# Low parts of the side weights made by ScalarE and an adding DMA from GpSimd, in place of a VectorE subtraction

## Time and profile before

| | before |
|---|---|
| median of 3 runs | 2506.87 us (2506.82 to 2506.97) |
| span of the profiled execution | 2505.1 us |
| TensorE busy | 2490.8 us, 99% |
| TensorE weight loads | 2204.3 us, 88% |
| VectorE busy | 1961.7 us, 78% |
| ScalarE busy | 1232.5 us, 49% |
| GpSimd busy | 305.3 us, 12% |
| granted TensorE clock | 1.00 |
| DMA | 246.87 MB, 33.9% of 16 engines on SP's queue |

### The profile page before, as it was taken

The page is one execution under the profiler, slowest core; times in us unless marked ns, Lnnn a source line. Parts: engine busy times, 40 slices in busy tenths (PEclk is TensorE's granted clock), DMA queues, the critical chain, the costliest instruction groups (busy, mean ns, idle before and its releaser), DMA issues.

```text
span 2505.1 us, 37038 instructions
## 1 busy us (share of the span) xinstructions
PE 2490.8 (99%) x14548; PEld 2204.3 (88%) x14548; DVE 1961.7 (78%) x2794; ACT 1232.5 (49%) x1963; POOL 305.3 (12%) x250
## 2 busy tenths in 40 slices
PE   9999999999999999999999999999999999999998
PEld 7999988889999889999888899998888888899997
DVE  7878867778888688887777888876899786877663
ACT  6444445444444454444553544445577535644442
POOL 4000001320000000000023100000187221200002
PEclk9999999999999999999999999999999999999999
DMA  5333332223333423333323233334333333233331
GB/s 157 98 96 100 100 105 84 82 85 102 96 108 102 118 79 104 96 106 114 102 64 95 74 103 105 104 104 135 91 72 82 126 92 111 83 108 99 99 100 59
DMA packets 487299, 246.87 MB, mean 99 GB/s; under 512 B 42321, under 2 KB 483926, under 8 KB 486870
## 3 DMA queue, kind: packets, MB, share of 16 engines
q1 hardware_dynamic: 486674, 244.19, 33.9%
q10 hardware_dynamic: 452, 0.32, 0.1%
HBM read 240.27 MB, written 4.19 MB: 98 GB/s over the span
## 4 chain that ended last, share of the span: by engine, by line
PE 96%; DVE 2%; ACT 1%; DMA 0%; issue 0%; POOL 0%; DVEq 0%; ACTq 0%
PE bank L886 8%; PE bank L885 8%; PE bank L884 8%; PE bank L767 6%; PE bank L768 6%; PE bank L769 6%; PE psS L906 4%; PE psS L907 4%; PE psS L908 4%; PE psT L950 2%; PE psT L952 2%; PE psT L951 2%; PE psT L767 2%; PE psT L769 2%; PE psT L768 2%; PE bank L1449 1%
## 5 line engine op out<-in xcount | busy, mean ns | idle before, releaser
L2254 DVE TENSOR_TENSOR wlo<-raw,whi 128x1024 fp32r<-128x1024 f32 (+2 forms) x212 | 288.7, 1364 | 49.9 <-ACT whi L1575 46.7
L767 PE MATMUL bank<-xhi,whi 128*128 128x512 f32 x672 | 264.5, 394 | 0.0
L768 PE MATMUL bank<-xlo,whi 128*128 128x512 f32 x672 | 261.9, 390 | 0.0
L769 PE MATMUL bank<-xhi,wlo 128*128 128x512 f32 x672 | 261.8, 390 | 0.0
L884 PE MATMUL bank<-xsh,whi 128*128 128x256 f32 x840 | 237.8, 283 | 0.0
L885 PE MATMUL bank<-xsl,whi 128*128 128x256 f32 x840 | 237.7, 283 | 0.0
L886 PE MATMUL bank<-xsh,wlo 128*128 128x256 f32 x840 | 237.7, 283 | 0.0
L1575 ACT ACTIVATE whi<-raw 128x1024 fp32r<-128x1024 f32 (+2 forms) x209 | 214.5, 1030 | 39.1 <-PE bank L769 22.1
L2317 DVE TENSOR_TENSOR wlo<-tw,whi 128x1024 fp32r<-128x1024 f32 x140 | 171.6, 1226 | 63.4 <-ACT whi L1615 63.3
L906 PE MATMUL psS<-hhi,whi 128*128 128x512 f32 x488 | 191.7, 393 | 0.0
L907 PE MATMUL psS<-hlo,whi 128*128 128x512 f32 x488 | 191.6, 393 | 0.0
(11 more groups left out here) (709 smaller groups left out, 7280.5 us busy)
## 6 DMA issues: line engine op xcount, KB each, us to landing
raw<-in_ffn_wg SPq DMA_DIRECT2D x88, 512.0 KB
raw<-in_ffn_wu SPq DMA_DIRECT2D x88, 512.0 KB
raw<-in_w_in SPq DMA_DIRECT2D x53, 512.0 KB
raw<-in_w_mlp SPq DMA_DIRECT2D x40, 512.0 KB
raw<-in_ffn_wd SPq DMA_DIRECT2D x48, 256.0 KB
raw<-in_ffn_wd SPq DMA_DIRECT2D x24, 448.0 KB
raw<-in_ffn_wd SPq DMA_DIRECT2D x48, 192.0 KB
raw<-in_ffn_wd SPq DMA_DIRECT2D x48, 128.0 KB
```

Of the source, the lines that this page charges most:

```text
L767: pe.matmul(dest, a, rhs_hi(k), start=start and k == 0, stop=False)
L768: pe.matmul(dest, a, rhs_lo(k), start=False, stop=False)
L769: mm = pe.matmul(dest, b_, rhs_hi(k), start=False, stop=stop and k == tiles - 1)
L2254: dve.tensor_tensor(wlo[:, a:a + n], raw[:, a:a + n], whi[:, a:a + n].bitcast(F32), ALU.subtract).then_inc(s_split, 1)
```

## The change

VectorE's `whole_lo` goes, in the networks and the MLP. Right behind `whole_hi`, ScalarE writes a second pass over the same raw columns, scaled by -1, into `wlo`: the negated high part. GpSimd then issues a DMA that adds the raw columns to it in place, from SBUF to SBUF, so that `wlo` holds raw minus high. There is one such DMA for each side, 164 in all; it waits for the pass by `k_nh`, and its landing raises `k_sl[0]` or `k_sl[1]` by 16. TensorE waits for that before a side; SP waits for it before it loads the next rows into the slot, since the DMA reads `raw` till then. VectorE's other increments of `s_split` are raised so that the count of four per window stays (`weight_sums` adds 2 from the second window on, the first split after the windows adds 2); `k_lo` counts three per window. GpSimd's DMA loop stands before the mixing stage of each layer, after its sums of squares, and before the last norm's sums for the MLP.

To have semaphores for this, four of the memory's norm are merged with four of the attention's v path, with offsets in their waits; that moves no instruction.

```
 def side_rows(w, i):                          # SP
     slot_free(c, q0)
+    if w:
+        sp.wait_ge(k_sl[i], 16 * (net.first_g + w))
...
 for m in range(KC):
+    if m in (2, 3):
+        sp.wait_ge(k_sl[m - 2], 16 * (net.first_g + FAST))
     down_rows(LAST_AT + m, -1, m)
...
 def fast_window(w):                           # TensorE
-    pe.wait_ge(k_lo, 4 * g + 1)
+    pe.wait_ge(k_lo, 3 * g + 1)
...
-    pe.wait_ge(k_lo, 4 * g + 3)
+    pe.wait_ge(k_sl[0], 16 * (g + 1))
     side(w, 0).then_inc(s_used, 1)
...
-    pe.wait_ge(s_split, q + c + 4 + RING)
+    pe.wait_ge(k_sl[1], 16 * (g + 1))
     side(w, 1).then_inc(s_used, 1)
...
 def whole_hi(j, i):                           # ScalarE
     act.activation(whi[:, a:a + n], raw[:, b_:b_ + n], ACT.Copy).then_inc(s_hi, 1)
+    act.activation(wlo[:, a:a + n], raw[:, b_:b_ + n], ACT.Copy, scale=-1.0).then_inc(k_nh, 1)
...
 def weight_sums(j):                           # VectorE
-    dve.tensor_tensor(tw[:, 3 * S:4 * S], raw[:, S:UNIT], tw[:, 0:S], ALU.subtract).then_inc(s_split, 1)
+    dve.tensor_tensor(tw[:, 3 * S:4 * S], raw[:, S:UNIT], tw[:, 0:S], ALU.subtract
+                      ).then_inc(s_split, 2 if j else 1)
...
-def whole_lo(j, i):
-    dve.wait_ge(s_hi, q0 + c0 + 4 * (PLAIN + j) + 2 + 2 * i)
-    a, b_, n = (2 * i + 1) * UNIT, (2 + i) * UNIT, side_cols(j, i)
-    dve.tensor_tensor(wlo[:, a:a + n], raw[:, b_:b_ + n], whi[:, a:a + n].bitcast(F32),
-                      ALU.subtract).then_inc(s_split if i else k_lo, 1)
...
+def sides_lo(first, cols):                    # GpSimd
+    for w in range(len(cols)):
+        for i in range(2):
+            a, b_, n = (2 * i + 1) * UNIT, (2 + i) * UNIT, cols[w][i]
+            pool.wait_ge(k_nh, 2 * (first + w) + i + 1)
+            pool.dma_start(wlo[:, a:a + n], raw[:, b_:b_ + n], accum_op=ALU.add).then_inc(k_sl[i], 16)
...
 for l in range(0, L):
+    net_sides_lo(2 * l)
     mix(l)
     squares(l * 3 + 2)
+    net_sides_lo(2 * l + 1)
...
+sides_lo(FIRST_G, [[len(MSIDES[w, i]) * P for i in range(2)] for w in range(MFAST)])
 squares(FINAL1 + 3, FINAL1 + 3, KC - 1, more=1)
```

More of the change, by code:

```diff
@@ L332, in build @@
         a_os = sem("attn_out_low_rest")
[L333 to L336, removed]
+        s_vs = sem("v_scaled_or_mem_normed")
+        s_vt = sem("v_or_mem_transposed")
+        s_vh = sem("vhi_ready_or_mem_squared_or_root")
+        s_vl = sem("vlo_ready_or_mem_newton_step")
         s_qs = sem("qk_scaled")
@@ L450, in build @@
         k_lo = sem("fast_weights_lo_ready")
+        k_nh = sem("side_weights_hi_negated")
+        k_sl = [sem(f"side_weights_lo_landed{i}") for i in range(2)]
         k_pe = sem("fast_product_done")
@@ L480, in build @@
         assert (C_MLP + WINDOWS_AT) % RING == 0
+        SIDE_SLOTS = (2, 3)
         FIRST_G, FIRST_ADD = sum(net.fast for net in NETS), 2 * L * ADDS
@@ L727, in mlp_side_rows @@
                 slot_free(c, 0)
+                if w > 0:
+                    sp.wait_ge(k_sl[i], 16 * (FIRST_G + w))
                 chunks = sorted({(grp, m) for grp, m, k in MSIDES[w, i]})
@@ L746, in _ @@
             for m in range(KC):
-                load(C_MLP + MLAST_AT + m, 0, c2(t["w_mlp2_2"], *MGROUPS[-1], m * P))
+                c = C_MLP + MLAST_AT + m
+                slot_free(c, 0)
+                if slot(c) in SIDE_SLOTS and m < RING:
+                    sp.wait_ge(k_sl[SIDE_SLOTS.index(slot(c))], 16 * (FIRST_G + MFAST))
+                sp.dma_start(dst(c, 0, mlp_tiles(-1)), c2(t["w_mlp2_2"], *MGROUPS[-1], m * P)
+                             ).then_inc(landed[slot(c)], LANDED)
             ov = out.rearrange("o (i p) d -> p (o i) d", p=P)
@@ L1303, in _ @@
                     r = m // 5
-                    pe.wait_ge(s_mn, MB)
+                    pe.wait_ge(s_vs, L + MB)
                     if r:
@@ L1312, in _ @@
                                               memr[:, j * D + cc * P:j * D + (cc + 1) * P], ident[:, :])
-                    mm.then_inc(s_mt, 1)
+                    mm.then_inc(s_vt, 1)
             def cross_q(h, ready=None):
@@ L1485, in mlp_window @@
                 mlp_terms(bank_d, cwh, cwl, S, mlp_corner(4, 0), True, True).then_inc(k_pe, 1)
-                pe.wait_ge(k_lo, 4 * g + 2)
+                pe.wait_ge(k_lo, 3 * g + 2)
                 pe.wait_ge(k_sn, 3 * g + 1)
@@ L1495, in mlp_window @@
                 mlp_terms(bank_c, whi, wlo, S, mlp_summed(0), True, True).then_inc(s_used, 1)
-                pe.wait_ge(k_lo, 4 * g + 4)
+                pe.wait_ge(k_lo, 3 * g + 3)
                 pe.wait_ge(k_sn, 3 * g + 2)
                 mlp_terms(bank_a, whi, wlo, 2 * UNIT, mlp_summed(2), False, True, True).then_inc(k_pe, 1)
-                pe.wait_ge(k_lo, 4 * g + 3)
+                pe.wait_ge(k_sl[0], 16 * (g + 1))
                 mlp_side(w, 0).then_inc(s_used, 1)
@@ L2035, in _ @@
                                            accum_out=st2[:, 16 + i:17 + i])
-                    e.then_inc(s_mr, 1)
-                    act.wait_ge(s_mst, 1)
-                    act.activation(st2[:, 20:22], st2[:, 18:20], ACT.Sqrt).then_inc(s_mr, 1)
+                    e.then_inc(s_vh, 1)
+                    act.wait_ge(s_vl, L + 1)
+                    act.activation(st2[:, 20:22], st2[:, 18:20], ACT.Sqrt).then_inc(s_vh, 1)
                 if m in (3, 6):
                     r = m // 6
-                    act.wait_ge(s_mt, r + 1)
+                    act.wait_ge(s_vt, L + r + 1)
                     for i in range(4):
@@ L2249, in _, with split @@
         def _(dve):
-            def split(c, q, tiles=8):
+            def split(c, q, tiles=8, units=1):
                 dve.wait_ge(s_hi, q + c + 1)
@@ L2333, in ahead @@
                     elif u == 4 * PLAIN + 1:
-                        whole_lo(0, 0)
+                        pass
                     elif u == 4 * PLAIN + 2:
@@ L2338, in ahead @@
                     else:
-                        split(c0 + u, q0, UNIT_TILES.get(u, 8))
+                        split(c0 + u, q0, UNIT_TILES.get(u, 8), 2 if u == LAST_AT else 1)
                 def quarter_sums(i):
@@ L2424, in fast_window @@
                     side_adds(w, 0)
-                    if on:
-                        whole_lo(w + 1, 0)
-                    else:
+                    if not on:
                         ahead(u + 5)
@@ L2906, in _ @@
                     v, y = st2[:, 18:20], st2[:, 20:22]
[L2907 to L2910, removed]
+                    dve.wait_ge(s_vh, L + 1)
+                    dve.tensor_scalar(v, st2[:, 16:18], 1.0 / D, EPS, ALU.mult, ALU.add).then_inc(s_vl, 1)
+                    dve.wait_ge(s_vh, L + 2)
+                    dve.reciprocal(y, y).then_inc(s_vl, 1)
                     for j in range(2):
[L2912 to L2918, removed]
+                        dve.wait_ge(s_vl, L + j + 2)
+                        dve.tensor_tensor(v, v, y, ALU.mult).then_inc(s_vl, 1)
+                    dve.wait_ge(s_vl, L + 4)
+                    dve.tensor_scalar(v, v, -0.5, 1.5, ALU.mult, ALU.add).then_inc(s_vl, 1)
+                    dve.wait_ge(s_vl, L + 5)
+                    dve.tensor_tensor(y, v, y, ALU.mult).then_inc(s_vl, 1)
+                    dve.wait_ge(s_vl, L + 6)
                     for i in range(MB):
                         mr = memr[:, i * D:(i + 1) * D]
-                        dve.tensor_scalar(mr, mr, st2[:, 20 + i:21 + i], None, ALU.mult).then_inc(s_mn, 1)
+                        dve.tensor_scalar(mr, mr, st2[:, 20 + i:21 + i], None, ALU.mult).then_inc(s_vs, 1)
                 if m in (3, 6):
@@ L3071, in mlp_sums_lo @@
                                   ALU.subtract).then_inc(k_lo, 1)
[L3073 to L3077, removed]
             def mlp_last_lo(j):
@@ L3086, in mlp_ahead @@
                 elif u < MLAST_AT + KC:
-                    split(C_MLP + u, 0)
+                    split(C_MLP + u, 0, 8, 2 if u == MLAST_AT else 1)
             def mlp_quarter_sums(i):
@@ L3138, in mlp_window @@
                 mlp_side_adds(w, 0)
-                if on:
-                    mlp_whole_lo(w + 1, 0)
-                else:
+                if not on:
                     mlp_ahead(MLAST_AT + 1)
@@ L3179, in _ @@
             mlp_hidden_lo(MPLAIN - 2, tmp[2])
-            mlp_whole_lo(0, 0)
             mlp_sums_lo(0, 1)
@@ L3313, in _, with net_sides_lo @@
             pool.wait_ge(s_ro, 13)
+            def sides_lo(first, cols):
[4 more added lines that the diff above has]
+                        pool.dma_start(wlo[:, a:a + n], raw[:, b_:b_ + n], accum_op=ALU.add).then_inc(k_sl[i], 16)
+            def net_sides_lo(nf):
+                net = NETS[nf]
+                sides_lo(net.first_g, [[net.side_cols(w, i) for i in range(2)] for w in range(net.fast)])
             for l in range(0, L):
+                net_sides_lo(2 * l)
                 mix(l)
                 squares(l * 3 + 2)
+                net_sides_lo(2 * l + 1)
             pool.wait_ge(s_x, (FINAL1 + 1) * KC)
```

14 lines of the change are left out of this document (4 added, 10 removed).

## The result

The changed kernel takes 2510.78 us (median of 20 runs, 2510.58 to 2511.05) against 2506.89 us before (20 runs, 2506.70 to 2507.15): +3.9 us, a ratio of 1.0016 with a 95% interval of 1.0009 to 1.0022. That is inside the 0.2% that the prediction counts as no change, but on the slower side, 3.8 us above the forecast of 2507.0, and its interval leaves out a ratio of 1. The span went from 2505.1 to 2509.0 us.

A forecast was written before the change was run, and what follows sets the result against it. TensorE, busy 2490.8 of 2505.1 us, was taken as the bound. Sum: 2505.1 + 0 (VectorE) + 0.1 (ScalarE in the MLP) + 0 (transfers) + 1.8 outside the span = 2507.0 us, no change; range 2505.3 to 2512.9 us.

The forecast's parts named there:

- VectorE: Side subtractions removed, 114.4 us of VectorE time beside a TensorE that never waits for it: gain 0, at best 1.6 us.
- The rival in which it reaches the end: VectorE's relief closes more than its own four waits: 2505.3 us by those waits; chance of over 0.2% faster 0.03.
- ScalarE in the networks: Second pass for side 1 delays the copy of TensorE's first block to 211.68, wanted at 212.18: hidden by 0.5 us, cost 0.
- ScalarE in the MLP: Copy behind the second pass ends 0.11 us before the third block; bounds 0 and 1.1 us over 11 windows, 0.1 taken.
- Transfers: 164 adding DMAs from GpSimd land before TensorE wants the low part: cost 0, at the upper bound about 6.0 us.
- L: Time from the end of ScalarE's second pass to the transfer's landing: 5.5 us, between 2.5 and 9.4.
- GpSimd's own share: GpSimd's part of the time from second pass to landing: 1.4 us, between nothing and 2.8 us.
- Loads: SP's queue waits for landings and transfers slow weight loads by at most 1.8 us; VectorE's weight sums covered by 6.6: cost 0.
- The late landing: Rival: landing exceeds what TensorE leaves; nothing to 7.8 us, every window pays beyond 10.8, 2663 us at 12; chance 0.06.
- hold GpSimd up: Rival: GpSimd writes descriptors only while VectorE idles, delaying side 0's transfer start by 5.7 us: 2520 us, chance 0.03.
- The first DMA: Rival: GpSimd's queue setup lengthens TensorE's first wait and moves everything one for one: 2512 us, chance 0.02.
- Windows still without a wait of TensorE: Sign that the prediction is right: in the windows, TensorE still shows no waits after the change.

The follow-up runs named there:

- late_all: Changed kernel with ScalarE's second pass for side 1 moved behind the copies TensorE waits for, in all windows including the first ones: 2506.43 us, ratio 0.9998 to before.
- late_first: Changed kernel with ScalarE's second pass for side 1 moved behind the next corner's pass and third block's copy in the four first windows alone: 2508.86 us, ratio 1.0008.
- double_dma: Changed kernel with each of the 164 adding transfers issued twice, the second after the first landed, TensorE and SP waiting for the second: 2523.18 us, ratio 1.0075.
- dma_alone: Changed kernel with its transfers but without ScalarE's second pass; VectorE writes the negated high part instead: 2506.43 us, ratio 0.9998 to before.
- double_other: Against double_dma, the second transfer adds the high part instead of the raw weights, and SP waits only for the first landing: 2560.77 us, ratio 1.0212.

## Why the prediction was right or wrong

**VectorE: right.** Its relief gave nothing: late_all has it, and its time can't be told from that of the kernel before. The rival in which it reaches the end did not happen.

**ScalarE in the networks: the term that failed.** The prediction gave 0, "hidden by 0.5 us", from one window, and that window follows one with four tiles in side 1. The same working on the window at 674, 674.76 + 2 x 0.61 + 0.37 = 676.35, ends 0.15 us past the third block's start at 676.20: 2.1 us in 14 windows. Measured, 2.4. That the two are so close is in part luck: the passes overlap, so the copy ends some 0.2 us earlier than this sum has it, and TensorE starts 0.15 us after the copy's end, not at it. The mechanism, the copy behind the pass, was named; what failed was to let one window stand for 66, in which the copy of the changed kernel ends between 0.14 and 0.86 us ahead of the third block. For the first windows the prediction worked out the transfer alone and left out what stands behind the pass on ScalarE there: 2.15 us by the starts, 1.9 us by late_first.

**The range: held by luck.** The measured time lies inside it, but its high end stands on late landings in the first windows (6.0 us), which did not happen. What filled 3.8 us of it is ScalarE in the networks, to which the sum gave 0 without bounds.

**ScalarE in the MLP: right, at the better bound.** 0.1 taken, 0 measured. The pass began 0.09 us before the one ahead of it had ended, as the prediction took into account when it chose, and the copy 0.10 us before the pass had; so the copy ends 0.35 us ahead of the third block, where the sum without overlap had it 0.11.

**Transfers: right, and near in size.** L, from the end of the pass to the landing, was 5.5 us with bounds of 2.5 and 9.4; it measures 3.2 to 6.4 us, in the middle 3.8 (side 0) and 4.7 (side 1). GpSimd's own share was the mis-sized half, 1.4 us taken; issue begins 0.29 us after the pass, and what follows takes 4.2 (4.1 taken). TensorE's first use of a side comes at least 4.3 us after the landing. The estimate of 2.6 us by the Trainium skill's page "DMA: Bandwidth & Descriptors" (section "Anatomy of one DMA — SWDGE (gpsimd) path") is too low for an adding transfer within SBUF: 4.1 us for 256 KB in the trace, and the measurement decides.

**Loads: right that they cost nothing, wrong about the cover.** SP waited for landings 67 times in the networks, and TensorE not once for what followed. But one more transfer, some 4 us, already cost 12.4 us, through the very chain for which the prediction gave 6.6 us of cover.

**The rivals.** The late landing did not happen; its price curve, nothing until 7.8 us, is too kind, since the loads give way before TensorE meets the landing (double_dma). VectorE did not hold GpSimd up: the issue follows the pass by 0.29 to 0.62 us, while VectorE is as busy as before but for the subtractions it no longer makes. That two-tensor operations leave GpSimd free to write descriptors is what the Trainium skill's page "SBUF — State Buffer" (section "Who interferes with whom") says, with its reason marked as inferred; the 0.29 us, and 0.85 to 1.06 us for every DMA instruction, agree. The first DMA cost no start: TensorE's first wait is 3.8 us as before.

**The signs to look for.** "Windows still without a wait of TensorE" was too coarse a test: the 14 stalls appear in no view of waits. VectorE 114 us lighter and ScalarE 104 us heavier took sums of groups for busy time; measured, 96.4 and 78.3.

## What to carry to other kernels

Work added to an engine with room is hidden only where nothing queued behind it is due: take the cover from the window that has the least of it, not from one that is at hand, and look for it where two lengths that vary (here a short side, then a long one) meet. The remedy is then order, not less work: the pass, moved behind the copies that TensorE waits for, cost nothing any more (late_all). And a loss near nothing can mark a cover that has just run out; doubling the suspect (3.9 us, then 46 us) shows it.

## What the runs showed of the hardware

An adding transfer from SBUF to SBUF, issued by GpSimd, keeps it 0.86 us and lands 2.9 to 6.1 us later, in the middle 4.1 us for 192 KB and 4.4 us for 512 KB: over this range the size hardly shows. The DMA engines' mean share over the windows of the first network goes up from 0.35 to 0.53 by these transfers (dma_alone), and that kernel lost no time that can be measured.

TensorE's granted clock fell after a wait. In double_other TensorE waited 2.25 us for a landing, until 262.50. Busy time of the engines in the stretches before, during and after (the columns as in the earlier trace rows):

```profile
256.00:259.90 3.90, 3.90 (x30) 3.65 (x29) 2.38 (x5) 2.82 (x5) 1.72 (x2) 1.00 0.52 144
259.90:262.40 2.50, 0.34 (x3) 0.14 (x2) 2.33 (x4) 1.10 (x3) 0.00 (x0) 1.00 1.11 221
262.40:265.00 2.60, 2.50 (x6) 1.95 (x7) 1.91 (x3) 0.63 (x1) 0.38 (x1) 0.56 0.20 41
265.00:269.00 4.00, 4.00 (x28) 3.72 (x26) 0.69 (x1) 1.32 (x3) 1.37 (x2) 0.86 0.94 236
```

The clock is 0.56 in the 2.6 us behind the wait, so mostly at its lower level of 1.2 GHz, and comes back after that: six matmuls where the full clock has some eleven. In the changed kernel, whose stalls stay under 0.8 us in the windows, it stays at 1.0.
